# Attention with exponentials kept in PSUM, the scale folded into the queries and the maximum taken with its sign

## The reference

```python
# first block: 4 heads of width 256 over a memory of 256 rows
s = einsum("bshd,bmhd->bhsm", qh, kh) * (1.0 / sqrt(HEAD_DIM))
pr = softmax(s, axis=-1)
o = einsum("bhsm,bmhd->bshd", pr, vh)
# second block, even layer: 8 heads of 64 (2 key heads), then 8 heads of 96
sc = einsum('bkgqd,bksd->bkgqs', qblk, kt) * scale      # 64**-0.5, 96**-0.5
p = softmax(sc, axis=-1); o = einsum('bkgqs,bksd->bkgqd', p, vt)
# second block, odd layer: 16 heads of 64, a window of 8 x 16 keys and a bias per head
sc = einsum('bhqd,bhqkd->bhqk', qblk, kg) * 64**-0.5 + bias
p = softmax(sc, axis=-1); o = einsum('bhqk,bhqkd->bhqd', p, vg)
```

## Time and profile before

| | |
|---|---|
| three runs | 1295.30, 1298.03, 1300.07 us, median 1298.03 |
| profiled execution | 1297.04 us, of which the span of the core 1294.9 |
| granted TensorE clock, mean | 0.967 of 2.4 GHz |
| busy: PE, weight load, VectorE, ScalarE, GpSimd | 1199.2, 1110.5, 877.6, 619.6, 375.7 us |
| HBM traffic | 155 GB/s over the span |
| chain that ended last, by engine | PE 76%, DVE 16%, ACT 5% |

### The profile page before, as it was taken

How to read it: one execution, slowest core, us unless ns; L and a number is a source line. 1 busy time by engine, 2 the same in 40 slices (tenths; PEclk the granted TensorE clock), 3 DMA queues, 4 the chain that set the end, 5 groups by cost and what they waited for, 6 DMA issues and landing times.

```text
span 1294.9 us, 20581 instructions
## 1 busy us (share of the span) xinstructions
PE 1199.2 (93%) x8047; PEld 1110.5 (86%) x8047; DVE 877.6 (68%) x1114; ACT 619.6 (48%) x824; POOL 375.7 (29%) x312
## 2 busy tenths in 40 slices
PE   4999889999899999999867889999999988999997
PEld 4999789999799899999766779999989777999996
DVE  3677998988466688888768846555565485555554
ACT  5554324344453454554657645444453474544442
POOL 1009999801300312222212414880010130100000
PEclk9999999999799999999978799999999979999999
DMA  8453445565226555554343028655555502555550
GB/s 268 162 179 131 146 139 183 165 195 190 70 98 189 164 183 176 190 193 164 113 139 130 1 66 235 195 195 184 179 164 190 193 1 71 188 180 182 193 192 35
DMA packets 139427, 201.01 MB, mean 155 GB/s; under 512 B 3252, under 2 KB 119988, under 8 KB 139372
## 3 DMA queue, kind: packets, MB, share of 16 engines
q1 hardware_dynamic: 138128, 195.83, 46.1%
q0 software_dynamic: 912, 3.17, 1.0%
q10 hardware_dynamic: 332, 1.25, 0.3%
HBM read 199.20 MB, written 1.05 MB: 155 GB/s over the span
## 4 chain that ended last, share of the span: by engine, by line
PE 76%; DVE 16%; ACT 5%; issue 2%; POOL 1%; DMA 1%; POOLq 0%; ACTq 0%; SPq 0%; DVEq 0%
PE ps L1456 70%; DVE wlo L896 4%; DVE work L1039 4%; PE ps L1555 4%; ACT whi L511 2%; PE ps L1591 1%; DVE work L996 1%; DVE work L1091 1%; ACT p_hi L531 1%; DMA x<-in_x 1%; POOL q_lo L395 1%; DVE stat L986 1%; DVE work L1206 0%; DVE stat L983 0%; DVE misc L976 0%
## 5 line engine op out<-in xcount | busy, mean ns | idle before, releaser
L896 DVE TENSOR_TENSOR wlo<-raw,whi 128x2048 fp32r<-128x2048 f32 x174 | 405.4, 2333 | 216.4 <-ACT whi L511 216.3
L511 ACT ACTIVATE whi<-raw 128x2048 fp32r<-128x2048 f32 x189 | 361.0, 1915 | 277.3 <-PE ps L1456 272.2
L1456 PE MATMUL ps<-p_hi,whi 128*128 128x256 f32 x1632 | 466.5, 286 | 23.3 <-DVE wlo L896 18.6
L1456 PE MATMUL ps<-p_lo,whi 128*128 128x256 f32 x1632 | 464.9, 285 | 0.0
L1456 PE MATMUL ps<-p_hi,wlo 128*128 128x256 f32 x1632 | 464.7, 285 | 0.0
L1456 PEld LDWEIGHTS ps<-p_hi,whi 128*128 128x128 f32 x1632 | 316.2, 194 | 28.2 <-DVE wlo L896 12.4
L1456 PEld LDWEIGHTS ps<-p_lo,whi 128*128 128x128 f32 x1632 | 316.4, 194 | 1.5
L1456 PEld LDWEIGHTS ps<-p_hi,wlo 128*128 128x128 f32 x1632 | 316.3, 194 | 0.0
L1456 PE MATMUL ps<-whi,q_hi 128*128 128x512 f32 x376 | 147.3, 392 | 3.5 <-DVE wlo L896 2.0
L401 POOL TENSOR_TENSOR wlo<-raw,whi 128x2048 fp32r<-128x2048 f32 x15 | 69.5, 4637 | 276.9 <-ACT whi L511 276.9
L1456 PE MATMUL ps<-whi,q_lo 128*128 128x512 f32 x376 | 146.8, 390 | 0.0
(11 more groups left out here) (229 smaller groups left out, 1672.7 us busy)
## 6 DMA issues: line engine op xcount, KB each, us to landing
raw<-in_w_in SPq DMA_DIRECT2D x36, 1024.0 KB, 5.0
raw<-in_w_up SPq DMA_DIRECT2D x22, 1024.0 KB, 5.1
raw<-in_up_a SPq DMA_DIRECT2D x16, 1024.0 KB, 5.5
raw<-in_down_a SPq DMA_DIRECT2D x16, 1024.0 KB, 4.9
raw<-in_up_b SPq DMA_DIRECT2D x16, 1024.0 KB, 5.4
raw<-in_down_b SPq DMA_DIRECT2D x16, 1024.0 KB, 4.9
raw<-in_od_w_qkv SPq DMA_DIRECT2D x12, 1024.0 KB, 5.2
raw<-in_w_down SPq DMA_DIRECT2D x11, 1024.0 KB, 5.0
```

The costliest lines, as they stand in the source:

```text
L511: nc.scalar.activation(whi[:, g % R, :], raw[:, g % R, :], ACT.Copy).then_inc(hi_ready, 1)
L896: nc.vector.tensor_tensor(wlo[:, g % R, :], raw[:, g % R, :], whi[:, g % R, :].bitcast(F32), ALU.subtract).then_inc(lo_ready[g % R], 1)
L1456: ins = nc.tensor.matmul(dst, lhs, rhs, start=first and n == 0, stop=last and n == 2)
```

## The change

- The scale is multiplied into the queries where they are copied out of PSUM: in ScalarE's copies for att1 and att2, in VectorE's multiply for att3. There the factor is also negative, so PSUM holds the negative of the scores.
- The maximum comes out negated: in att1 and att2 by `negate=True` of the reduce; in att3 the bias table is built negated, and the running operation is a minimum of negative sums. The multiply of line 986 is gone, and with it the semaphore `at_max`.
- The exponentials are written back to the PSUM bank of the scores, for att3 too. The reciprocal is multiplied onto both tiles by one tensor_tensor, which reads PSUM and writes `prob` in SBUF.
- `scores(i)` waits for that product of head i-2. The wait of ScalarE for the transposes goes to VectorE, ahead of the product.

```diff
# GpSimd, bias table
-                nc.gpsimd.tensor_copy(bias[:, h], rev).then_inc(bias_step, 1)
+                nc.gpsimd.tensor_scalar(bias[:, h], rev, -1.0, None, ALU.mult).then_inc(bias_step, 1)
-    ...affine_select(out=part, in_=part, compare_op=ALU.is_ge, fill=NEG, base=base,
+    ...affine_select(out=part, in_=part, compare_op=ALU.is_ge, fill=FAR, base=base,
# ScalarE, attention
                         act.wait_ge(at_nm, n + 1)
-                        if i >= 3:
-                            act.wait_ge(at_t, n - 2)
                         for t in range(T):
                             src = bsc[:, i % 2, t, :] if biased else bank(i % 2, t * S, t * S + S)
-                            last = nc.scalar.activation(prob[:, i % 3, t, :], src, ACT.Exp,
+                            last = nc.scalar.activation(bank(i % 2, t * S, t * S + S), src, ACT.Exp,
                                                         bias=att_nmax[...],
-                                                        scale=1.0 if biased else scale(i),
+                                                        scale=-1.0 if biased else 1.0,
                                                         accum_out=att_sum[...])
# ScalarE, queries out of PSUM (att1; att2 alike with HD or B_QK ** -0.5)
-                nc.scalar.activation(qreg[...], bank(2), ACT.Copy).then_inc(bank_read[2], 1)
+                nc.scalar.activation(qreg[...], bank(2), ACT.Copy,
+                                     scale=MEM_HD ** -0.5).then_inc(bank_read[2], 1)
# VectorE, attention
                                 last = nc.vector.tensor_tensor_reduce(
                                     out=bsc[:, i % 2, t, :], in0=both[:, t, :], in1=bias[...],
-                                    scale=1.0, scalar=NEG, op0=ALU.add, op1=ALU.max,
-                                    accum_out=att_max[...])
-                            last.then_inc(at_max, 1)
+                                    scale=1.0, scalar=FAR, op0=ALU.add, op1=ALU.min,
+                                    accum_out=att_nmax[...])
+                            last.then_inc(at_nm, 1)
                         else:
-                            nc.vector.tensor_reduce(out=att_max[:, pair], in_=both, axis=AX.X, op=ALU.max)\
-                                .then_inc(at_max, 1)
-                        dve.wait_ge(at_max, n + 1)
-                        nc.vector.tensor_scalar(att_nmax[:, pair], att_max[:, pair],
-                                                -1.0 if biased else -scale(i), None, ALU.mult).then_inc(at_nm, 1)
+                            nc.vector.tensor_reduce(out=att_nmax[:, pair], in_=both, axis=AX.X, op=ALU.max,
+                                                    negate=True).then_inc(at_nm, 1)
                     if 1 <= i <= N:
                         dve.wait_ge(at_e, n)
...
                         nc.vector.reciprocal(inv, sums).then_inc(at_rs, 1)
                         dve.wait_ge(at_rs, n)
-                        for t in range(T):
-                            rows = prob[:, (i - 1) % 3, t, :]
-                            last = nc.vector.tensor_scalar(rows, rows, att_rs[...], None, ALU.mult)
-                        last.then_inc(at_p, 1)
+                        if i >= 4:
+                            dve.wait_ge(at_t, n - 3)
+                        nc.vector.tensor_tensor(prob[:, (i - 1) % 3], ps[:, (i - 1) % 2, :]...,
+                                                inv.to_broadcast([P, T, S]), ALU.mult).then_inc(at_p, 1)
# VectorE, queries and keys of att3
-                    ... scalar=HD ** -0.5 if i < 4 else 1.0,
+                    ... scalar=-(HD ** -0.5) if i < 4 else 1.0,
# TensorE, scores(i) for i >= 2
-                    pe.wait_ge(at_max if biased else at_e, n0 + i - 1)
+                    pe.wait_ge(at_p, n0 + i - 1)
```

More of the change, by code:

```diff
@@ L49 @@
 RPB_H, RPB_W = 15, 31
-NEG = -1.0e30
+FAR = 1.0e30
 V_CONVB, V_CONVA, V_MIX, V_MEM, V_GATE, V_CBIAS, V_LNG, V_LNB, V_FFN = 0, 31, 34, 35, 36, 39, 40, 41, 42
@@ L144, in two_blocks @@
         mhalf = stat[:, 54:74]
-        att_max, att_nmax = stat[:, 74:78], stat[:, 78:82]
+        att_nmax = stat[:, 74:78]
         att_sum, att_rs = stat[:, 82:114], stat[:, 114:146]
@@ L210, in two_blocks @@
         mg, mg_hi, mg_lo = sem("mg"), sem("mg_hi"), sem("mg_lo")
-        at_s, at_max, at_nm, at_e = sem("at_s"), sem("at_max"), sem("at_nm"), sem("at_e")
+        at_s, at_nm, at_e = sem("at_s"), sem("at_nm"), sem("at_e")
         at_rs, at_p, at_t, at_h, at_v = sem("at_rs"), sem("at_p"), sem("at_t"), sem("at_h"), sem("at_v")
@@ L255, in two_blocks @@
         ATT = {
-            "att1": (heads_mem(), 1, 0, 0, lambda i: MEM_HD ** -0.5, False, 0),
-            "att2": (heads_even(), 2, 4, 4, lambda i: (HD if i < A_HEADS else B_QK) ** -0.5, False, 1),
-            "att3": (heads_odd(), 2, 12, 20, lambda i: HD ** -0.5, True, 2),
+            "att1": (heads_mem(), 1, 0, 0, False, 0),
+            "att2": (heads_even(), 2, 4, 4, False, 1),
+            "att3": (heads_odd(), 2, 12, 20, True, 2),
         }
@@ L404, in attention @@
             def attention(name):
-                units, H, u0, n0, scale, biased, k = ATT[name]
+                units, H, u0, n0, biased, k = ATT[name]
                 if H == 1:
@@ L487, in _ @@
                         pool.wait_ge(bias_step, steps)
-                        nc.gpsimd.affine_select(out=part, in_=part, compare_op=ALU.is_ge, fill=NEG, base=base,
+                        nc.gpsimd.affine_select(out=part, in_=part, compare_op=ALU.is_ge, fill=FAR, base=base,
                                                 pattern=[[0, 6], [sign, 48]], channel_multiplier=-sign)\
@@ L636, in _ @@
                 act.wait_ge(slot_used, G_UGQ + 3 + 3 * i)
-                nc.scalar.activation(qreg[:, bass.ds(BW * i, BW)], bank(2), ACT.Copy).then_inc(bank_read[2], 1)
+                nc.scalar.activation(qreg[:, bass.ds(BW * i, BW)], bank(2), ACT.Copy,
+                                     scale=MEM_HD ** -0.5).then_inc(bank_read[2], 1)
                 hi(G_UGQ + 5, i)
@@ L814, in _ @@
                 src = ps[0:B_QK, b, :] if i > 2 else bank(b, 0, n)
-                nc.scalar.activation(dst, src, ACT.Copy).then_inc(bank_read[b], 1)
+                by = HD ** -0.5 if i < 2 else B_QK ** -0.5 if 2 < i < 7 else 1.0
+                nc.scalar.activation(dst, src, ACT.Copy, scale=by).then_inc(bank_read[b], 1)
                 if i == 2:
@@ L978, in attention @@
                                     in1=bias[:, i, 2 - 2 * t:6 - 2 * t, :].rearrange("p j k -> p (j k)"),
-                                    scale=1.0, scalar=NEG, op0=ALU.add, op1=ALU.max,
-                                    accum_out=att_max[:, 2 * (i % 2) + t:2 * (i % 2) + t + 1])
-                            last.then_inc(at_max, 1)
-                        else:
-                            nc.vector.tensor_reduce(out=att_max[:, pair], in_=both, axis=AX.X, op=ALU.max)\
-                                .then_inc(at_max, 1)
-                        dve.wait_ge(at_max, n + 1)
-                        nc.vector.tensor_scalar(att_nmax[:, pair], att_max[:, pair],
-                                                -1.0 if biased else -scale(i), None, ALU.mult).then_inc(at_nm, 1)
+                                    scale=1.0, scalar=FAR, op0=ALU.add, op1=ALU.min,
+                                    accum_out=att_nmax[:, 2 * (i % 2) + t:2 * (i % 2) + t + 1])
+                            last.then_inc(at_nm, 1)
+                        else:
+                            nc.vector.tensor_reduce(out=att_nmax[:, pair], in_=both, axis=AX.X, op=ALU.max,
+                                                    negate=True).then_inc(at_nm, 1)
                     if 1 <= i <= N:
@@ L993, in attention @@
                         dve.wait_ge(at_rs, n)
-                        for t in range(T):
-                            rows = prob[:, (i - 1) % 3, t, :]
-                            last = nc.vector.tensor_scalar(rows, rows, att_rs[:, 16 * t + i - 1:16 * t + i], None,
-                                                           ALU.mult)
-                        last.then_inc(at_p, 1)
+                        if i >= 4:
+                            dve.wait_ge(at_t, n - 3)
+                        nc.vector.tensor_tensor(prob[:, (i - 1) % 3], ps[:, (i - 1) % 2, :].rearrange("p (t n) -> p t n", t=T),
+                                                inv.to_broadcast([P, T, S]), ALU.mult).then_inc(at_p, 1)
                     if i >= 3:
@@ L1428, in _ @@
                     out=reg[:, BW * (i % 4):BW * (i % 4) + BW].rearrange("p (h n) -> p h n", h=2),
-                    in0=ps[:, i % 4, :].rearrange("p (h n) -> p h n", h=2), scalar=HD ** -0.5 if i < 4 else 1.0,
+                    in0=ps[:, i % 4, :].rearrange("p (h n) -> p h n", h=2), scalar=-(HD ** -0.5) if i < 4 else 1.0,
                     in1=beside, op0=ALU.mult, op1=ALU.mult).then_inc(bank_read[i % 4], 1)
```

## The result

| | before | after |
|---|---|---|
| median, 20 runs each | 1297.08 us | 1303.56 us |
| lowest and highest | 1291.97, 1300.58 | 1297.95, 1310.72 |
| ratio after to before | | 1.0056 [1.0037, 1.0075] |
| profiled execution, its span | 1297.04, 1294.9 | 1305.37, 1303.2 |
| mean granted clock in it | 0.967 | 0.955 |

The changed kernel is 0.56% slower, about 7 us. The forecast was 1299.5 us and no measurable change; the range of 1290 to 1309 holds the median. The 20 runs after fall into two groups: ten of 1297.95 to 1301.88 us at mean clocks of 0.961 to 0.967, and ten of 1305.23 to 1310.72 at 0.953 to 0.958. The first lie where the forecast does, the others near rival C's 1305.5 and rival B's 1311. The profiled execution is one of the second group.

The account below looks back on a forecast made before the run. TensorE was taken as the bound at the low clock, VectorE's pace at full clock, then the closed loop. Att1 +0.8, att2 -0.9 and att3 +2.1 gave +2.0 us: 1299.0 or 1300.0 by base, so 1299.5; range 1290 to 1309.

Parts of the forecast that it names:

- rival C: In the attentions, the product is still held up by GpSimd or takes 1.0 us: +6 us, 1305.5; chance 0.09.
- rival B: Clock falls or stays at 0.50 for one whole attention more, TensorE idling in heads and starts: +9.5 us, 1311; chance 0.17.
- The closed loop: Scores, maximum, product, next scores set each full-clock head: 2.55 us in att2 (-2.0 in all), 2.71 in att3 (+0.7).
- The product: VectorE's one 512-element multiply out of PSUM per head: 0.69 us, bounds 0.62 and 1.0, not disturbed by GpSimd.
- The exponentials: ScalarE's exponentials written to PSUM: taken at 0 change, bounds -0.1 and +0.2 us each, exposed only at the three starts.
- The starts: First heads, pipeline empty, scores wait for the product: S(5), head 5's scores, +1.6 us in att2, +1.9 in att3.
- The tails: Behind the last maximum the small multiply falls away: -0.5 us each in att2 and att3, nothing in att1.
- GpSimd's bias table: GpSimd's 16 bias copies become multiplies by -1: at worst 32 us more, hidden in its idle time.
- Rival A: In the attentions the new wait is hidden, heads run at TensorE's 2.1 and 2.2 us: -9.5 us, 1288.5; chance 0.17.
- The sum: Over the three attentions: att1 +0.8, att2 -0.9, att3 +2.1, together +2.0 us, giving 1299.5.
- the forecast's own path: Whole kernel without the rivals: 1295 to 1304 us, four heads' clock either way less what cancels; chance 0.45.
- att1's start: In att1 only head 2's scores are exposed to the wait: +0.8 us, handed on as one chain at the low clock.

Follow-up runs that it names:

- e7_wait_late: e3_one_product_sbuf with the scores waiting for the product of head i-2 from head 5 on only; 1296.3 us, 1.0011 of before.
- e6_wait_starts: e3_one_product_sbuf with the scores waiting for the product in heads 2, 3 and 4 of each attention only; 1302.8 us, 1.0038 of before.
- e3_one_product_sbuf: The changed kernel with exponentials in SBUF, one product within SBUF and the old release of the scores; 1289.8 us, 0.9936 of before.
- e5_wait_all: e3_one_product_sbuf with the scores waiting for the product of head i-2 in all three attentions; 1308.3 us, 1.0104 of before.

## Why the prediction was right, and where it was not

- **The closed loop.** Forecast 2.55 us in att2 and 2.71 in att3. Measured 2.63, and 2.71 to 2.72. The 0.08 of att2 is the step from product to scores, 0.14 us of issue where 0.05 was taken from the earlier trace rows; in att3 it is made up by smaller errors. Right.
- **The product** was taken as 0.69 and undisturbed: 0.690 to 0.692 in 36 heads. Rival C is refuted in both its forms.
- **The exponentials** were taken at no change. They were 0.03 us shorter each, which the earlier trace rows could not show. The Trainium skill (ScalarE: Activation LUTs, "Step-by-step: what each stage is for") says that ScalarE writes to PSUM faster, and these runs agree: 0.445 against 0.472 us.
- **The starts.** In att2, S(5) began 13.3 us after R(0), 1.9 later than before, where 1.6 was forecast. In att3, S(5) came 10.67 us after S(2), before 8.47: 2.2 later, forecast 1.9. TensorE's timeline of att3 after, the first score matmuls of heads 2 to 5:

```profile
1036.21 0.58 PE L1551 MATMUL ps<-p_hi 64*128 64x256 f32 x1 [2.29 <-POOL p_lo L395]
...
1039.63 0.55 PE L1551 MATMUL ps<-p_hi 64*128 64x256 f32 x1 [0.72 <-DVE work L993]
...
1043.01 0.55 PE L1551 MATMUL ps<-q_hi 64*128 64x256 f32 x1 [0.72 <-DVE work L993]
...
1046.88 0.58 PE L1551 MATMUL ps<-q_hi 64*128 64x256 f32 x1
```

- **The tails** were forecast at -0.5 each. From the last maximum to the last value matmul att2 went from 7.60 to 7.14 us and att3 from 7.81 to 7.24.
- **GpSimd's bias table** took 11 us more in sum and cost nothing that shows, as forecast.
- **Rival A** is refuted: the wait is the chain in every full-clock head, and alone it costs 17 to 19 us.
- **The sum.** +2.0 us was forecast. At equal H, after stands at 1297.4 and before at 1295.5: +1.9, or +1.2 with the slope of 0.35, within that reckoning's 1 us. The sum was right as a sum over the engines' work.
- **Rival B's time** was added up wrongly: +9.5 us on 1299.5 is 1309, not 1311. The range ends there all the same.

What failed is the choice between the forecast and **rival B**. The sum took att2 and att3 to have as many heads at the low level as before; the prediction gave B, "stays at 0.50 for one whole attention more", 0.17. In ten of the 20 runs something near it happened, with mean clocks of 0.953 to 0.958, under the 0.96 that the prediction named as the sign of B; in the profiled execution it was six heads of 3.90 us in att3 against about three. Between the means of the runs, 1296.8 and 1303.9 us, H rose by 16.7 us: 16.7 x 0.31 = 5.2 us of the 7.1, and the +1.9 is what this leaves. The median, 1303.56 us, falls between the two groups and just inside the 1295 to 1304 of the forecast's own path; that it does is in part luck. The place was named, the weight was too small: the waits at the starts, each lengthened, were reckoned as delays and not as what also decides how long the level behind them stays low. And of B's two reasons, the idle 0.45 us in each head and the gaps between the first heads, only the second is borne out, by e7_wait_late against e6_wait_starts. The longer gaps did not bring about the fall itself in att3: there the first matmul of S(2), at 1036.21, already took 0.58 us, behind a gap of 2.29 us that before has as well (2.30), and the longer waits ahead of S(3) and S(4) came after it. What differs is the stay, worked out from the granted clock of short stretches: from about 1037.5 to 1051.2 us before, and from 1036.2 to 1070.3 after.

One term was mis-sized: **att1's start**, +0.8. In the profiled executions the stretch from the norm's matmuls to the first output matmul went from 35.11 to 37.95 us, +2.8. The wait before S(2) came out near the forecast, +0.94 from the norm's matmuls on. But it was not handed on: S(2) itself ran at the higher level for most of its matmuls, 0.28 us each for the 0.41 of before, and that gave 0.74 back. What arrived is the clock: the 32 small matmuls behind head 0's transposes took 4.03 us at a granted clock of 0.88 before, and 6.83 at 0.50 after. TensorE's timeline, before and then after:

```profile
338.32 0.55 PE L1555 MATMUL ps<-p_hi 128*128 128x256 f32 x1 [1.47 <-ACT work L596]
...
341.55 4.03 PE L1621 MATMUL ps<-mean_w,misc 128*128 128x1 f32 x32
```

```profile
338.55 0.36 PE L1551 MATMUL ps<-p_hi 128*128 128x256 f32 x1 [2.22 <-DVE work L993]
...
341.04 6.83 PE L1617 MATMUL ps<-mean_w,misc 128*128 128x1 f32 x32
```

Whether this holds for all runs was not seen; each kernel has one trace.

Open: what in a start decides how many heads stay at 1.2 GHz. The small set of matmuls hardly changed it and the larger did, but no set between them was run, and the extra ones ahead of att1's and att2's first scores were not tried by themselves. Why after splits into two groups of equal size is open as well.

## What to carry to other kernels

Before a buffer is kept longer (here a PSUM bank, until the product has read it), write down the loop that its release closes and compare the loop's length with the busiest engine's work per turn; here, with two banks, there was nothing beside it. Then price the same wait a second time where the pipeline is still empty: here that start cost twice what the steady loop did, mostly through TensorE's clock. A change that takes work off an engine and adds a wait should be run in halves: the folding alone gained 6 us, and with the product and the wait added the whole lost 6.5.

## What the runs showed of the hardware

- TensorE, busy 27.99 of 28 us, from 1043 to 1071 in att3 of after, was granted 0.51 over that stretch, and left the lower level only at about 1070 us. Being busy did not bring it back for six heads.
- Two tensor_scalar multiplies within SBUF, 0.62 us undisturbed, took 3.09 and 3.16 us beside GpSimd; one product with a broadcast operand within SBUF took 0.69, and up to 1.70 in e3_one_product_sbuf and 1.73 in e5_wait_all; the same product out of PSUM was 0.690 to 0.692 in all 36 heads of after.
- GpSimd's multiply by an immediate took 1.18 us where its copy of the same 128x384 tile took 0.51.
- In a head of att2 the scores behind the product started 0.14 us after it ended, against 0.05 for transposes behind a subtraction. Why they differ was not tested.
